# Four chunks of the last modulation through ScalarE and accumulating DMAs, with two raw weight buffers for three, in an adaLN, attention, short-convolution and expert layer

## What is computed

```
sh1, sc1, g1, sh2, sc2, g2 = split(silu(cond) @ w_ada + b_ada, 6)   # w_ada: 2048 x (6*2048); two cond rows: context, latent
h    = rms_norm(x) * (1 + sc1) + sh1
q, k, v, bg, cg, u = split(h @ w_in)                                # 1024, 256, 256, 1024, 1024, 1024 columns
mixed = concat(rms_norm(attention(q, k, v)), rms_norm(bg * conv3(cg * u)))
x    = x + g1 * (mixed @ w_out)
h2   = rms_norm(x) * (1 + sc2) + sh2
x    = x + g2 * expert_choice_moe(h2)                               # 16 experts, 2048 -> 1024 -> 2048, 48 tokens each
```

## Time and profile before

| | |
|---|---|
| runs | 1526.66, 1526.85, 1529.8 us, median 1526.85 us |
| span of the profiled execution | 1525.0 us |
| what lies around the span | not shown for that execution; the median of the runs is 1.85 us above the span |
| PE / DVE / ACT / POOL busy | 1446.9 / 602.3 / 255.1 / 26.7 us |
| conv steps 0 to 23 | 182.6 to 452.1 us of the span |
| output projection | 452.1 to about 592 us |
| granted TensorE clock | 0.993 of full speed |

### The profile page before, as it was taken

How to read it: one execution, slowest core, us unless ns; L and a number is a source line. 1 busy time by engine, 2 the same in 40 slices (tenths; PEclk the granted TensorE clock), 3 DMA queues, 4 the chain that set the end, 5 groups by cost and what they waited for, 6 DMA issues and landing times.

```text
span 1525.0 us, 18551 instructions
## 1 busy us (share of the span) xinstructions
PE 1446.9 (95%) x7856; PEld 882.0 (58%) x7856; DVE 602.3 (39%) x1019; ACT 255.1 (17%) x358; POOL 26.7 (2%) x58
## 2 busy tenths in 40 slices
PE   6999999999999999999989989999889899899998
PEld 3667788888889997435435335335335335335433
DVE  4433977978768986101301301301301301211313
ACT  4233223333233223000000000000000000000200
POOL 0000000000000000000000000000000000000000
PEclk9999999999999999999999999999999999999999
DMA  9999688777787659999999999999999999999999
GB/s 374 403 395 325 263 324 316 268 261 260 276 294 273 221 191 366 371 433 434 430 431 433 427 435 431 431 434 428 435 431 430 434 429 435 431 429 431 431 422 349
DMA packets 99263, 572.48 MB, mean 375 GB/s; under 512 B 9532, under 2 KB 54532, under 8 KB 76676
## 3 DMA queue, kind: packets, MB, share of 16 engines
q1 hardware_dynamic: 87824, 520.14, 83.5%
q0 software_dynamic: 6912, 50.33, 8.6%
q10 hardware_dynamic: 4468, 1.14, 0.3%
HBM read 565.02 MB, written 6.55 MB: 375 GB/s over the span
## 4 chain that ended last, share of the span: by engine, by line
PE 66%; DMA 24%; DVE 5%; SPq 2%; issue 2%; ACT 1%; ACTq 0%; DVEq 0%
PE psum L639 64%; DMA ring<-in_w_up 20%; DMA ring<-in_w_ada 2%; SPq L551 2%; DMA res<-in_w_ada 1%; DVE res L1618 1%; DVE w_parts L1508 1%; DMA ring<-in_w_down 1%; PE psum L649 0%; PE psum L825 0%; PE psum L1077 0%; DVE stat L1578 0%; DVE hid L1577 0%; PE psum L1047 0%; DVE mix L1581 0%
## 5 line engine op out<-in xcount | busy, mean ns | idle before, releaser
L639 PE MATMUL psum<-ring,hid 128*64 128x512 f32 x3024 | 679.9, 596 | 54.0 <-DMA ring<-in_w_up 40.2
L639 PEld LDWEIGHTS psum<-ring,hid 128*64 128x64 f32 x3024 | 240.2, 138 | 470.3 <-issue 414.3
L1944 DVE TENSOR_TENSOR hid<-psum,hid 128x512 f32<-128x512 f32 x16 | 11.1, 691 | 516.3 <-PE psum L639 516.3
L639 PE MATMUL psum<-h_parts,w_parts 128*128 128x384 f32 x1152 | 207.3, 337 | 1.3 <-DVE mix L1651 1.3
L639 PEld LDWEIGHTS psum<-h_parts,w_parts 128*128 128x128 f32 x1152 | 199.9, 188 | 5.1 <-issue 2.5
L1508 DVE TENSOR_TENSOR w_parts<-ring,w_parts 128x2048 fp32r<-128x2048 f32 x52 | 119.0, 2289 | 76.4 <-ACT w_parts L1208 76.2
L1208 ACT ACTIVATE w_parts<-ring 128x2048 fp32r<-128x2048 f32 x52 | 99.6, 1916 | 209.0 <-PE psum L639 176.9
L639 PE MATMUL psum<-w_parts,h_parts 128*128 128x512 f32 x432 | 103.9, 395 | 2.8 <-DVE w_parts L1508 1.5
L639 PE MATMUL psum<-ring,early 128*32 128x512 f32 (+4 forms) x694 | 96.4, 536 | 7.8 <-DMA ring<-in_w_ada 6.0
L639 PEld LDWEIGHTS psum<-w_parts,h_parts 128*128 128x128 f32 x432 | 79.5, 188 | 28.5 <-issue 10.3
L639 PEld LDWEIGHTS psum<-early,mix 128*128 128x128 f32 x768 | 86.6, 192 | 9.0 <-issue 9.0
(11 more groups left out here) (216 smaller groups left out, 754.0 us busy)
## 6 DMA issues: line engine op xcount, KB each, us to landing
ring<-in_w_up SPq DMA_DIRECT2D x30, 4096.0 KB, 23.2
ring<-in_w_gate SPq DMA_DIRECT2D x28, 4096.0 KB, 30.4
ring<-in_w_down SPq DMA_DIRECT2D x26, 4096.0 KB, 30.0
ring<-in_w_ada POOLq DMA_DIRECT2D x48, 1024.0 KB, 7.5
ring<-in_w_in SPq DMA_DIRECT2D x36, 1024.0 KB, 8.3
ring<-in_w_ada SPq DMA_DIRECT2D x28, 768.0 KB, 15.6
res<-in_w_ada SPq DMA_DIRECT2D x16, 1024.0 KB, 5.7
ring<-in_w_out SPq DMA_DIRECT2D x16, 1024.0 KB, 5.8
```

What stands on the lines that cost most here:

```text
L639: return nc.tensor.matmul(out, lhsT, rhs, start=start, stop=stop, skip_group_check=True)
L1944: tt(by_row, bank[1][:, :].rearrange("p (b a) -> p a b", a=4), by_row, ALU.mult).then_inc(act_ready, 1)
```

## The change

It does four things. The four first chunks of modulation 5 leave TensorE: in eight jobs (a chunk and a half of its columns) SP loads 0.5 MB into `carry_in_buf`, ACT multiplies it with each of the two cond columns (128x1024 each), and POOL adds the two results to sums in DRAM by two accumulating DMAs. Job n stands in step 3n of SP and ACT (`CARRY_AT`). SP loads job n only when both DMAs of job n - 1 have landed (`carry_added`). The sums are loaded back to `added_up` (2 MB) in SP's step 27, before the first expert load, and DVE's first adds wait for that. To make room for the two small buffers, the raw weight buffers become two (`RAW = 2`). The order in which chunks of modulation 3 are loaded (the `s - 4` above) stays as it was.

```diff
-RAW = 3
+RAW = 2
...
-STREAM = [2, 4, 5]
-HERE = 4
-EVENT_SETS = [[(m, k) for k in range(first, min(first + 2, KC + 1))] for m in STREAM for first in range(0, KC + 1 if m < N_MOD - 1 else HERE, 2)]
+STREAM = [2, 4]
+EVENT_SETS = [[(m, k) for k in range(first, min(first + 2, KC + 1))] for m in STREAM for first in range(0, KC + 1, 2)]
-SETS_CONV = {s: 3 + n for n, s in enumerate([0, 1, 3, 4, 6, 7, 9, 10, 12, 13, 15, 16, 17, 18, 19, 21, 23])}
+SETS_CONV = {s: 3 + n for n, s in enumerate([0, 1, 3, 4, 6, 7, 9, 10, 12, 13, 15, 16, 17, 18, 19])}
...
-ADDED = range(HERE, KC)
+CARRIED = 4
+HALF = D // 2
+CARRY_JOBS = [(k, half) for k in range(CARRIED) for half in range(2)]
+CARRY_AT = {3 * n: n for n in range(len(CARRY_JOBS))}
+ADDED = range(CARRIED, KC)
...
+        carry_in_buf, carry_out_buf = ring[:, 3, 0:HALF], ring[:, 3, HALF:2 * HALF]
+        carry_sums = nc.dram_tensor("carry_sums", (2, P, D), F32).ap()
...
+            def carry_load(job):
+                k, half = CARRY_JOBS[job]
+                if job:
+                    sp.wait_ge(carry_added, 32 * job)
+                at = (N_MOD - 1) * D + half * HALF
+                sp.dma_start(carry_in_buf, ada_rows[k * P:(k + 1) * P, at:at + HALF]).then_inc(carry_in, 16)
...
+                if s in CARRY_AT:
+                    carry_load(CARRY_AT[s])
                 if s == CONV_ADDS[0]:
                     chunk_load(0)
                 if s in FIRST_AT:
                     sp.wait_ge(unit_used, U_QKV + U_CONV)
+                    if s == min(FIRST_AT):
+                        sp.wait_ge(carry_added, 32 * len(CARRY_JOBS))
+                        for n in range(2):
+                            sp.dma_start(added_up[n], carry_sums[n]).then_inc(carried_back, 16)
                     first_load(FIRST_AT[s])
                 if s - 4 in CONV_ADDS[:-1]:
                     chunk_load(CONV_ADDS.index(s - 4) + 1)
...
+            def carry_add(job):
+
+                k, half = CARRY_JOBS[job]
+                pool.wait_ge(carry_ready, job + 1)
+                for n, rows in enumerate((carry_out_buf, carry_in_buf)):
+                    sums = carry_sums[n][:, half * HALF:(half + 1) * HALF]
+                    if k == 0:
+                        pool.dma_start(sums, rows).then_inc(carry_added, 16)
+                    else:
+                        pool.dma_start(sums, rows, accum_op=ALU.add).then_inc(carry_added, 16)
...
+            places = [-1] * (len(SETS_Q) + len(SETS_KV)) + list(SETS_CONV)
+            for k in range(2):
+                ada_load(STREAM[0], k)
+            for place, events in zip(places, EVENT_SETS):
+                carry_until(place)
+                for m, k in events:
...
-            partition_sums(bank[0], added_up, False, ada_free)
+            pe.wait_ge(mod_read, N_MOD - 3)
+            partition_sums(bank[0], added_up, True, ada_free)
...
+                if s in CARRY_AT:
+                    job = CARRY_AT[s]
+                    k = CARRY_JOBS[job][0]
+                    a.wait_ge(carry_in, 16 * (job + 1))
+                    nc.scalar.activation(carry_out_buf, carry_in_buf, ACT.Copy, scale=cond[:, k, 0:1])
+                    nc.scalar.activation(carry_in_buf, carry_in_buf, ACT.Copy, scale=cond[:, k, 1:2]).then_inc(carry_ready, 1)
...
                     if i < 2:
-                        v.wait_ge(unit_used, U_QKV + U_CONV)
-                        ts(added_up[n], ada_buf[t % 2], cond[:, k, n:n + 1], None, ALU.mult).then_inc(add_done, 1)
+                        v.wait_ge(carried_back, 32)
                     else:
                         v.wait_ge(add_done, i - 1)
-                        stt(added_up[n], ada_buf[t % 2], cond[:, k, n:n + 1], added_up[n], ALU.mult, ALU.add).then_inc(add_done, 1)
+                    stt(added_up[n], ada_buf[t % 2], cond[:, k, n:n + 1], added_up[n], ALU.mult, ALU.add).then_inc(add_done, 1)
```

More of the change, by code:

```diff
@@ L73 @@
 X_PART = KC * T // X_PARTS
-ADDED = range(HERE, KC)
+CARRIED = 4
[3 more added lines that the diff above has]
+ADDED = range(CARRIED, KC)
 ADDS_AT = {s: 2 for s in (3, 4, 5, 7, 8, 9, 10, 11, 12, 13)} | {2: 1, 14: 3}
-ADA_USES = 2 * KC + HERE + 1
+ADA_USES = 2 * KC + 1
 BLOCKS = [(0, 768), (768, 768), (1536, 512)]
@@ L168, in parts_at @@
             return nc.alloc_sbuf_tensor_at(name, [P, n], F32R, offset=at)
-        raw = ring[:, 0:2, :].rearrange("p s n -> p (s n)")[:, 0:RAW * UNIT]
+        raw = ring[:, 0, 0:RAW * UNIT]
         w_parts = parts_at("w_parts", PARTS * 2 * UNIT, ring_at + 4 * RAW * UNIT)
@@ L342, in build @@
         x_saved, x_back, chunk_in, add_done_3, summed_3 = sem("x_saved"), sem("x_back"), sem("chunk_in"), sem("add_done_3"), sem("summed_3")
+        carry_in, carry_ready, carry_added, carried_back = sem("carry_in"), sem("carry_ready"), sem("carry_added"), sem("carried_back")
         moe_landed = [sem(f"moe_landed{n}") for n in range(WIDE)]
@@ L617, in _, with ada_load @@
             pool.wait_ge(w_used, len(PIECES))
-            def ada_load(m, k, j, added=False):
-                if added:
+            def ada_load(m, k):
+                j = k % 2
+                if k - 2 in ADDED and m == N_MOD - 1:
                     pool.wait_ge(add_done, 2 * (k - 2 - ADDED[0]) + 2)
+                elif m == N_MOD - 1:
+                    pool.wait_ge(ada_free, k - ADDED[0] + 2 * KC + 1)
                 else:
                     pool.wait_ge(ada_free, k + (KC * STREAM.index(m) + 1))
-                pool.dma_start(ada_buf[j], ada_rows[bass.ds(k * P, P), m * D:(m + 1) * D]).then_inc(ada_landed[j], 16)
@@ L626, in _ @@
[L626 to L631, removed]
+                pool.dma_start(ada_buf[j], ada_rows[k * P:(k + 1) * P, m * D:(m + 1) * D]).then_inc(ada_landed[j], 16)
+            def carry_add(job):
[7 more added lines that the diff above has]
+                        pool.dma_start(sums, rows, accum_op=ALU.add).then_inc(carry_added, 16)
@@ new lines, in _, with carry_until @@
+            jobs = [0]
+            def carry_until(place):
+                while jobs[0] < len(CARRY_JOBS) and 3 * jobs[0] <= place:
+                    carry_add(jobs[0])
+                    jobs[0] += 1
+            places = [-1] * (len(SETS_Q) + len(SETS_KV)) + list(SETS_CONV)
[4 more added lines that the diff above has]
+                for m, k in events:
+                    if k < KC:
+                        t = KC * STREAM.index(m) + k + 2
+                        if t < 2 * KC:
+                            ada_load(STREAM[t // KC], t % KC)
+                        else:
+                            ada_load(N_MOD - 1, ADDED[t - 2 * KC])
@@ L632, in _ @@
+            carry_until(U_CONV)
+            for k in ADDED[2:]:
+                ada_load(N_MOD - 1, k)
             pool.wait_ge(unit_used, U_ALL - 1)
@@ L1806, in ada_add @@
                     k, n = ADDED[i // 2], i % 2
-                    t = 2 * KC + k
+                    t = 2 * KC + k - ADDED[0]
                     v.wait_ge(ada_landed[t % 2], 16 * (t // 2 + 1))
                     if i < 2:
-                        v.wait_ge(unit_used, U_QKV + U_CONV)
-                        ts(added_up[n], ada_buf[t % 2], cond[:, k, n:n + 1], None, ALU.mult).then_inc(add_done, 1)
+                        v.wait_ge(carried_back, 32)
                     else:
                         v.wait_ge(add_done, i - 1)
-                        stt(added_up[n], ada_buf[t % 2], cond[:, k, n:n + 1], added_up[n], ALU.mult, ALU.add).then_inc(add_done, 1)
+                    stt(added_up[n], ada_buf[t % 2], cond[:, k, n:n + 1], added_up[n], ALU.mult, ALU.add).then_inc(add_done, 1)
                 adds[0] += count
```

## The result

The changed kernel takes **1636.49 us** (median of 4 runs, 1635.6 to 1639.41) against 1526.85, a ratio of 1.0717 [1.0704, 1.0730]: slower by 109.6 us. The profiled execution took 1635.82 us with a span of 1634.0.

A forecast was written before the change was run, and what follows sets the result against it. PE was taken to bound the kernel up to the routing, with DVE's chunk-add loop close behind. The terms -3.8 + 43 + 32 + 10 + 12 = +93 us on 1526.85 gave 1620 us, range 1565 to 1690.

The forecast's parts named there:

- two event sets off PE: Two event sets of 1.92 us each leave PE after steps 21 and 23, on the chain: -3.8 us.
- order of chunk loads with two buffers: Conv stage: chunk loads leave only after the low part of the step that adds them, so DVE and PE wait: +43 us.
- jobs' waits on SP's queue: Chunk loads queue behind SP's wait for the job before: +32 us in steps 3, 9, 15 and +10 in 6, 12, 18.
- traffic: Conv stage: 16 MB more of DMA lengthens twelve chunk landings by 1 us each: +12 us.
- one of the 3.3: Steps 6, 12 and 18: what sticks out of the job wait, 3.3 us each, three times, +10 us together.
- The loop: Conv stage: adds, low part, unit issue and chunk landing set a step of 15.5 us, 14.4 without attention.
- the 18.1: Time from the low part's end through ACT, POOL, the pair's landing and job load to the chunk's landing: 18.1 us.
- Edits costed at nothing: Later unit loads, ACT's scalings, POOL's event loads, DVE's second inputs and the sums' way back: no cost in the sum.
- Buffers only: Rival: jobs land quickly or their wait hides, the buffers alone cost: 1566, up to 1590 us; 20%.
- Slack swallowing the loop: Rival: slack between DVE and PE swallows most of the loop, jobs' waits count: 1568, down to 1540 us; 8%.
- The slow pair: Rival: the accumulating pair lands slowly (22.8 us) and sets the pace: 1712 us, deciding from about 15 on; 15%.
- PE alone: Rival: all waits are covered and only PE's removed event sets count: 1523 us, faster; 4%.

The follow-up runs named there:

- e9: e5 with all jobs of SP, ACT and POOL taken out, the four first chunks of modulation 5 left out and the two event sets still out: 1523.06 us.
- e5: The changed kernel with both moves, chunk loads ahead of the unit load and job loads (from job 1) two SP steps later: 1544.99 us.
- e4: The changed kernel with SP loading job n (from 1 on) in its step 3n + 2 instead of 3n, chunk loads as they were: 1593.27 us.
- e3: The changed kernel with each chunk load of modulation 3 issued ahead of its SP step's unit load, job loads as they were: 1553.49 us.
- e8: The kernel before with two raw buffers and each chunk load issued ahead of the unit load: 1526.43 us.
- e1: The kernel before with two raw buffers instead of three and nothing else changed: 1577.19 us.
- e7: e5 with plain stores of the same size for the accumulating DMAs, the products of chunks 0 to 2 left out: 1531.35 us.
- e10: e9 with the jobs' loads and ACT's sixteen scalings put back, but no DMA to DRAM and none back: 1523.40 us.

## Why the prediction was right, step by step

Forecast 1620 us and +93; measured 1636.5 and +109.6, inside the range of 1565 to 1690. The terms of the sum, beside the runs that measure them. The differences are taken along one way, from e9 over e5 and e4 to the change; on the way over e3 the order would have 83.0 and the jobs' waits 8.5, so the two rows belong together:

| step of the prediction | predicted | measured | from |
|---|---|---|---|
| two event sets off PE | -3.8 | -4.4 | e9; 3.4 between e8 and e9 |
| order of chunk loads with two buffers | +43 | +50.1 | e1; 48.3 between e4 and e5 |
| jobs' waits on SP's queue | +42 | +43.2 | the change less e4 |
| traffic | +12 | +21.9 | e5 less e9 |
| sum | +93 | +111 | 109.6 in all |

**What was luck.** The 90 us between steps 2 and 18 came out as forecast, with other shares than I gave them. The 16.5 that the forecast was short lie outside: 5.6 before step 2, where I had nothing in the sum, and 11.4 from step 18 on, where I had the sets' -3.8 and one of the 3.3; PE waited 3.4 us there in step 18 and 7.8 in step 20.

**The loop.** Its length was right, and that "the size of the buffer does not cost, the order does" is shown by e8. Undersized was how much of it reaches PE. In e1, by the starts of the second halves of steps 6, 12 and 18 (before: 250.22, and the starts in the earlier trace rows plus half of 8.7), the groups cost 20.3, 16.4 and 11.8 us, against 16.3, 15.9 and 10.9. In the first, the chunks of steps 2 and 3 landed in 10.3 and 12.5 us (205.35 to 215.64 and 222.90 to 235.40), not 7.1. And 2.7 more come behind the last of these starts, since the half behind the wait took 7.0 for 4.4. I had let the third group end where step 18 starts, but its wait falls into the step.

**The jobs' waits.** The sum was right partly by luck: errors cancel. I gave steps 3, 9 and 15 the same 10.6. By the starts of the adds they took 18.7 us (221.44 to 240.16), 30.1 and 30.7 (427.50 to 458.16), which is 4.3, 14.6 and 15.2 over the loop: 34.1 in place of 32. Against the same adds in e1, which has no jobs (19.8, 16.6 and 17.1), it is -1.0, 13.4 and 13.6: 26 in all, and nothing in step 3. Step 3 was cheap because the job it waits for is of chunk 0, whose pair is plain stores; those four landed in 2.9 to 5.2 us. I had priced them as accumulating. Steps 9 and 15 were dearer in two parts of the 18.1. From POOL's first issue to SP's release it took 10.3 (327.27 to 337.56), against 8.6. The chunk behind the job's load took 8.2, against 5.7: I had counted no transfer ahead of it, though the job's own load is one. All in all 22.7 us from the end of the low part (323.51) to the add. Steps 6, 12 and 18 were undersized: I had 3.3 for each. PE's timeline has waits of 6.2 and 7.8 us for the chunks behind steps 6 and 18, where e1 has none, with slower halves behind them:

```profile
304.73 5.96 PE L688 MATMUL psum<-h_parts,w_parts 128*128 128x384 f32 x24 [6.15 <-DVE hid L1701]
...
525.95 14.56 PE L688 MATMUL psum<-h_parts,w_parts 128*128 128x384 f32 x72 [7.76 <-DVE hid L1701]
```

From the start of step 7 to that of step 9 PE took 8.0 us more than in e1 (27.2 for 19.2), and from 13 to 15 7.2 more (32.33 for 25.18), of which 4.1 are waits for event loads. The 43.2 are less than these parts together, because e4 has costs of its own: there PE waits 9.6 us in step 18, for 4.3 in e1.

The Trainium skill's fit ("DMA: Bandwidth & Descriptors", the anatomy of a SWDGE DMA) gives 3.2 us for 0.5 MB by estimate. The four plain stores of the changed kernel agree, with a median of 3.4. The accumulating ones don't, with a median of 9.0. But they stand at other places: in e7, with plain stores at the places of the twelve accumulating ones, the median is 5.3 (2.9 to 8.2), against 8.2 (5.4 to 12.4) in e5, so the accumulation itself makes some 3 us of it. The two summaries of POOL's instructions, plain and then accumulating, in the changed kernel:

```profile
DMA to landing us min/median/max: 2.9/3.4/5.2
```

```profile
DMA to landing us min/median/max: 5.5/9.0/10.9
```

**Traffic** is the step that failed. As I put it, it would lengthen the twelve chunk landings by 1 us each. But from step 4 on the chunks behind unit loads landed in 6.9 to 8.3 us, and in e1 in 7.0 to 8.9 at the same places. Only that of step 2 was longer, 15.4 us (206.03 to 221.44) for 10.3 in e1. Of my 16 MB the page counts 8.4 MB more written (14.94 for 6.55) and 2.1 more read (567.11 for 565.02). Reads of the destination it does not show. Most of the cost was on POOL's queue, of which I had said that a set could wait only in step 0, for 0 to 4. There it did, and was 4.6: PE's two waits of 2.3 and 2.4 at 203.6 and 207.0, with a matmul step behind them of 10.2 us for 8.6.

```profile
203.59 1.07 PE L688 MATMUL psum<-ring,early 128*32 128x512 f32 x8 [2.27 <-DMA ring<-in_w_ada]
207.02 1.93 PE L688 MATMUL psum<-ring,early 128*32 128x512 f32 x8 [2.36 <-DMA ring<-in_w_ada]
```

In e5 such waits go on to 14.9 us, since loads behind an accumulating pair land late. I had counted POOL's `wait_ge` and not its pairs as what the loads stand behind. What part of the 21.9 us the changed kernel itself pays, where PE has slack from its other waits (8.7 us of event waits in all), is open.

**Edits costed at nothing.** ACT's scalings and the jobs' loads: nothing (e10 as e9). The unit loads one low part later: nothing (e8). The output projection and routing are 0.8 us longer, with its cause open.

**The rivals.** Buffers only (1566 to 1590) fell by e1 against the change, 59.3 us apart. Slack swallowing the loop (1540 to 1568) fell by e1's 50. The slow pair asked for a landing of 15 us and more, and the longest took 10.9. PE alone (1523) is what e9 gives, with the order mended and the jobs gone. The jobs with three raw buffers were not tried: there is no room for both.

## What to carry to other kernels

When the number of buffers changes, read every load that shares their queue by what it now stands behind: here the buffer was free, and a load written a few lines too low cost 50 us. Put the load with the least slack first and the wait for a slow store behind it, and price a wait in an issuing queue by what is queued behind it, not by its length. A work item moved off an engine that it occupied for 4 us must also be cheaper than that in the queues it is moved to.

## What the runs showed of the hardware

- An accumulating DMA of 0.5 MB to DRAM took POOL 0.88 to 1.21 us to issue, against 0.54 for a plain store, and landed in 5.5 to 10.9 us, against 2.9 to 5.2. Twelve plain stores at the same places (e7) landed in 2.9 to 8.2. Loads of 1 MB right behind an accumulating pair on the same queue landed in 11.0 to 14.2 in the changed kernel and in up to 16.3 in e5, against a median of 7.8 in the conv stage before.
- The granted clock fell where PE waited 3 to 21 us at a time, to between 0.79 and 0.94 in stretches of 47 to 62 us of the conv stage: for part of the time it was the lower of its levels, 1.2 and not 2.4 GHz. 24 matmuls behind such a wait took 5.9 to 7.3 us for 4.4. Filling the waits brought most of it back and gained nothing, because another engine set the pace. The windows of the changed kernel around the longest wait (length, busy time of PE, PEld, DVE, ACT and POOL, granted clock, DMA share, GB/s), and in the output projection:

```profile
305.00:352.00 47.00, 24.64 (x130) 21.10 (x131) 18.77 (x26) 8.79 (x16) 2.87 (x4) 0.79 0.53 168
...
560.00:714.00 154.00, 152.26 (x944) 145.78 (x944) 134.16 (x159) 52.48 (x59) 5.53 (x11) 1.00 0.82 294
```
